# Reading the sampled outputs between two convolution taps, and a reordered start of the heads and of the sample turns, in a hybrid decoder step

## The reference

```
[cq | ckv | kr | z | xBC | dt | mq | g] = u @ w_in
A: latent attention, 8 heads, causal; the sampled tokens attend to a paged cache of 2048 old ones
B: conv of width 4 on xBC, silu; scan with state: y = C.S + ...; y = y + d_skip * x; gate by silu(z); norm
M: 4-head attention to 256 memory tokens
m  = sig(gA)*(oA@WoA) + sig(gB)*(oB@WoB) + sig(gM)*(oM@WoM);  x1 = LN(alpha*x + m@w_out)
y  = LN(alpha*x1 + relu(x1@w_up+b_up)^2 @ w_down + b_down)
```

## Time and profile before

| | us |
|---|---|
| median of 3 runs | 1730.83 |
| lowest, highest | 1729.92, 1733.96 |
| the profiled execution, its own time | 1732.98 |
| its span, first to last instruction | 1731.3 |

### The profile page before, as it was taken

One profiled execution on the slowest core, in us unless ns is written; L12 is line 12 of the kernel. 1 busy time (PEld: TensorE's weight loads), 2 busy tenths in 40 slices (PEclk: granted clock), 3 DMA queues, 4 the chain that ended last, 5 costly groups with the idle time before them and its releaser, 6 DMA issues.

```text
span 1731.3 us, 25873 instructions
## 1 busy us (share of the span) xinstructions
PE 1670.3 (96%) x10438; PEld 1411.0 (82%) x10438; DVE 760.8 (44%) x1312; ACT 408.3 (24%) x800; POOL 405.7 (23%) x344
## 2 busy tenths in 40 slices
PE   8999999999999999999999999999997999999995
PEld 6868777787877777777777767779996999999995
DVE  5567678675341211111221213343477871067334
ACT  2252433425211111111111101132224111111122
POOL 0041221404120000000333210013444443333432
PEclk9999999999999999999999999999998999999998
DMA  5324233252262222212677764432331222322211
GB/s 195 142 80 171 68 117 128 93 178 79 100 210 72 73 61 73 61 62 76 225 240 246 239 244 180 174 131 88 96 98 37 86 86 86 90 94 86 86 62 52
DMA packets 70409, 206.23 MB, mean 119 GB/s; under 512 B 10161, under 2 KB 26802, under 8 KB 65682
## 3 DMA queue, kind: packets, MB, share of 16 engines
q1 hardware_dynamic: 50384, 151.67, 26.8%
q10 hardware_dynamic: 13762, 31.93, 5.4%
q0 software_dynamic: 6144, 20.98, 3.9%
HBM read 189.68 MB, written 14.86 MB: 118 GB/s over the span
## 4 chain that ended last, share of the span: by engine, by line
PE 86%; DVE 8%; ACT 2%; DMA 2%; issue 2%; SPq 1%; POOLq 0%; POOL 0%; ACTq 0%; DVEq 0%
PE acc L1724 30%; PE acc L1764 29%; PE acc L2064 6%; PE acc L2030 3%; PE acc L2012 2%; PE acc L2167 1%; PE bank L2079 1%; PE bank L2098 1%; PE bank L2080 1%; DVE work L1212 1%; PE bank L2181 1%; PE bank L2049 1%; PE bank L2055 1%; PE bank L2252 1%; PE bank L1933 1%
## 5 line engine op out<-in xcount | busy, mean ns | idle before, releaser
L1724 PE MATMUL acc<-xt,ring 128*128 128x272 f32 x2272 | 546.7, 398 | 2.8 <-DMA ring<-in_stream 2.8
L1724 PEld LDWEIGHTS acc<-xt,ring 128*128 128x128 f32 x2272 | 428.6, 191 | 103.9 <-issue 18.6
L1764 PE MATMUL acc<-x_parts,f_parts 128*128 128x272 f32 x1408 | 220.9, 293 | 12.0 <-DVE x_parts L1141 10.8
L522 POOL TENSOR_TENSOR f_parts<-ring,f_parts 128x1024 fp32r<-128x1024 f32 x65 | 157.7, 2425 | 247.9 <-ACT f_parts L701 247.7
L1764 PEld LDWEIGHTS acc<-x_parts,f_parts 128*128 128x128 f32 x1408 | 197.5, 192 | 14.5 <-issue 8.0
L500 POOL DMA_DIRECT2D work<-in_page_cols x128 | 68.8, 538 | 474.4 <-PE bank L2119 365.3
L1764 PE MATMUL acc<-f_parts 128*128 128x272 f32 x1344 | 172.3, 289 | 0.0
L1764 PEld LDWEIGHTS acc<-f_parts 128*128 128x128 f32 x1344 | 170.4, 188 | 0.1
L701 ACT ACTIVATE f_parts<-ring 128x1024 fp32r<-128x1024 f32 x65 | 69.0, 1061 | 238.4 <-PE acc L1764 204.3
L2064 PE MATMUL acc<-branch,ring 128*128 128x272 f32 x512 | 120.0, 392 | 0.0
L2064 PEld LDWEIGHTS acc<-branch,ring 128*128 128x128 f32 x512 | 96.0, 190 | 18.8
(11 more groups left out here) (351 smaller groups left out, 2044.8 us busy)
## 6 DMA issues: line engine op xcount, KB each, us to landing
ring<-in_stream SPq DMA_DIRECT2D x216, 512.0 KB, 3.6
work<-in_page_cols POOLq DMA_DIRECT2D x128, 160.0 KB, 3.3
attended<-in_ssm_state ACTq DMA_DIRECT2D x8, 1024.0 KB, 6.3
work<-cum_rows SPq DMA_DIRECT2D x32, 256.0 KB, 4.6
out_ssm_s<-attended ACTq DMA_DIRECT2D x8, 1024.0 KB, 5.5
work<-in_ckv_rows ACTq DMA_DIRECT2D x64, 128.0 KB, 3.6
work<-in_ckv_rows SPq DMA_DIRECT2D x64, 128.0 KB, 3.0
work<-in_memk_cols SPq DMA_DIRECT2D x8, 1024.0 KB, 6.5
```

The source lines that it names most:

```text
L522: pool.tensor_tensor(lo, ring[:, s * BLOCK:(s + 1) * BLOCK], hi.bitcast(F), SUB).then_inc(sem["split_ready"], 1)
L1724: m = pe.matmul(acc[p][:, half, 0:width], w[:, k * P:(k + 1) * P], x(kk)[:, half * width:(half + 1) * width], start=kk == 0, stop=kk == n_ ...
L1764: m = pe.matmul(acc_half, w[:, k * P:(k + 1) * P], x[:, kk, of], start=kk == 0 and n == 0, stop=kk == last and n == 2)
```

## The change

Four edits, no arithmetic changed.

1. VectorE, groups 0 to 3: the read of the sampled outputs (line 1401) moves from behind `finish` of chunk 0 into the convolution of chunk 1, between its second and third tap operation of line 1212's loop (before `i == 2`). In group 3, where there is no convolution, it runs at the same place as a plain call.
2. SyncE: the first two weight blocks of the sample turns are loaded ahead of the first turn's rows; three instead of five follow them.
3. VectorE: the wait for all heads' sampled queries, the memset and `queries(0)` move ahead of the last head's merge (line 1510).
4. TensorE: the wait for `new_read` moves from ahead of `queries(0)` to behind its 24 matmuls, where the later heads wait for `q_lat_read`.

```diff
-            load(blocks_before("sample") - blocks_before("mem_k"))
+            load(blocks_before("sample") - blocks_before("mem_k") + 2)
...
             cached_rows(0)
-            load(5)
+            load(3)
...
-            def conv(g, q):
+            def conv(g, q, between=None):
...
                 for i in range(1, CONV_W):
+                    if i == 2 and between:
+                        between()
                     signal = "conv_done" if i == CONV_W - 1 else "dve_step"
...
-                def ahead(q):
+                def ahead(q, between=None):
                     if g < GROUPS - 1:
-                        conv(g + 1, q)
+                        conv(g + 1, q, between)
+                    elif between:
+                        between()
...
+                def read_y_s():
+                    dve.wait_ge(sem["y_s_ready"], t.next("y_s_ready"))
+                    for hp in range(GC):
+                        y = BR[:, g * GC + hp, SEQ:T]
+                        m = dve.scalar_tensor_tensor(out=y, in0=y, scalar=skip_of(hp), in1=bank[3][:,
+                                hp * NS:(hp + 1) * NS], op0=MUL, op1=ADD)
+                    m.then_inc(sem["y_s_read"], 1)
...
                 read_y(1)
-                ahead(1)
+                ahead(1, between=read_y_s)
                 ahead_finish(0)
-                dve.wait_ge(sem["y_s_ready"], t.next("y_s_ready"))
-                for hp in range(GC):
-                    y = BR[:, g * GC + hp, SEQ:T]
-                    m = dve.scalar_tensor_tensor(out=y, in0=y, scalar=skip_of(hp), in1=bank[3][:,
-                            hp * NS:(hp + 1) * NS], op0=MUL, op1=ADD)
-                m.then_inc(sem["y_s_read"], 1)
...
                 if h < MLA_HEADS - 1:
                     read_q_lat(h + 1)
+                else:
+                    dve.wait_ge(sem["q_lat_read"], t.next("q_lat_read", MLA_HEADS))
+                    dve.memset(q_rot_b, 0.0).then_inc(sem["dve_step"], 1)
+                    dve.wait_ge(sem["dve_step"], t.next("dve_step"))
+                    queries(0)
                 t.skip("acc0_ready"), t.skip("acc0_free")
...
-            dve.wait_ge(sem["q_lat_read"], t.next("q_lat_read", MLA_HEADS))
-            dve.memset(q_rot_b, 0.0).then_inc(sem["dve_step"], 1)
-            dve.wait_ge(sem["dve_step"], t.next("dve_step"))
-            queries(0)
...
             m.then_inc(sem["new_turned"], 1)
-            pe.wait_ge(sem["new_read"], t.next("new_read"))
...
                 pe.wait_ge(sem["acc0_free"], t.value("acc0_free") + 1)
-                if h:
-                    pe.wait_ge(sem["q_lat_read"], t.next("q_lat_read"))
+                pe.wait_ge(sem["q_lat_read" if h else "new_read"], t.next("q_lat_read" if h else "new_read"))
```

More of the change, by code:

```diff
@@ L1488, in read_q_lat, with queries @@
                         t=DEC_SEQ)).then_inc(sem["q_lat_read"], 1)
+            def queries(b):
+                one = bass.ds(b, 1)
+                for c in range(2):
+                    dve.tensor_scalar(q_lat_b[:, c, :], q_lat[:, c, one, :, :].rearrange("p b h t -> p (b h t)"),
+                            1.0, None, MUL).then_inc(sem["dve_step"], 1)
+                    dve.wait_ge(sem["dve_step"], t.next("dve_step"))
+                for h in range(2):
+                    of = slice(h * ROPE, (h + 1) * ROPE)
+                    signal = "batch_q_ready" if h else "dve_step"
+                    dve.tensor_scalar(q_rot_b[of, h, :], q_rot[of, one, :, :].rearrange("p b h t -> p (b h t)"),
+                            1.0, None, MUL).then_inc(sem[signal], 1)
+                    dve.wait_ge(sem[signal], t.next(signal))
             rotate_q()
```

## The result

| | before | after |
|---|---|---|
| median us | 1732.39 (4 runs, 1729.92 to 1733.99) | 1714.96 (4 runs, 1714.35 to 1717.8) |
| profiled execution, its own time | 1732.98 | 1717.8 |
| its span | 1731.3 | 1716.1 |

The ratio is 0.9902, with an interval of 0.9889 to 0.9914: 17.4 us less. Forecast were 1714.5, between 1709.5 and 1720.5. The profiled execution of after is the slowest of its four, 2.8 us over their median, and its gain over the profiled one of before is 15.2 us.

A forecast was written before the change was run, and what follows sets the result against it. TensorE, busy 1670.3 of 1731.3 us, bounds the kernel; only its stalls and lower-clock stretches can be won. 7.4 + 2.5 + 7.7 = 17.6 us gives 1715.4 (profiled) or 1713.2 (median); taken 1714.5, range 1709.5 to 1720.5.

The forecast's parts named there:

- part 1: SSM stage, sampled outputs read between the taps: state products stop waiting, 8.6 us less 3 x 0.4, so 7.4 us.
- part 2: Start of the heads, wait for new latents behind the first 24 matmuls: 2.5 us gained.
- part 3: Sample turns' start: first queries 1.9, weight loads 2.8, first projection at full clock 3.0; 7.7 us in sum.
- I take 0.4: SSM groups 0 to 2: VectorE's lateness returns as a wait for state sums, 0.4 us a group, range to 1.0.
- the 2.78 of group 1: SSM group 1: 2.78 us more than group 3 between projection half starts, counted as gain besides 1.17 of lower clock.
- rival 1: TensorE's clock losses move to remaining gaps instead of going: 13.4 us gained, 1719.6 us; chance 0.12.
- its cover: Heads' start: 24 matmuls take 5.77 us, ending near 505.0, so the latents' copy at 501.75 is in time.
- Both clock terms of the prediction: Lower-clock losses counted as gains: 1.2 us in SSM group 1 and 3.0 us in the first turn's projection.
- (2): Second sample turn: its key loads become the bound, wait of 1.7 plus up to 3.0 us, 1720.1; chance 0.06.
- (3): Line 1918: VectorE gives the SSM read's gain back at the next group's start, all 7.4 us, 1722.8; chance 0.05.
- (4): Slower than before: shifted work meets the clock monitor badly, 3.0 us per projection, eight give 1739; chance 0.02.
- (5): The moved read waits for something new or moved loads block SyncE's queue; only part 2 holds, 1730.5; chance 0.02.

The follow-up runs named there:

- e7: The changed kernel with the sampled-output read one tap earlier, ahead of tap 1: 1717.58 us, ratio 0.9909.
- e3: The kernel before with only the two weight-block loads moved ahead of the first sample turn's rows: 1727.65 us, ratio 0.9977.
- e4: The kernel before with only the first queries (wait, memset, queries(0)) moved ahead of the last head's merge: 1732.73 us, ratio 1.0003.
- e2: The kernel before with only the wait for the new latents moved behind the heads' first 24 matmuls: 1727.21 us, ratio 0.9968.
- e1: The kernel before with only the sampled-output read moved between the convolution's taps: 1724.99 us, ratio 0.9952.
- e6: The changed kernel with the sampled-output read behind all three taps, still ahead of chunk 0's finish: 1720.52 us, ratio 0.9928.
- a2: The changed kernel run again without edit: 1715.66 us, ratio 0.9906 against the kernel before.
- e9: e8 with TensorE's wait for the last memory values moved behind the first memory head's projection: 1711.67 us, ratio 0.9876.
- a3: The changed kernel run a third time without edit: 1714.98 us, ratio 0.9898 against the kernel before.
- e8: The changed kernel with the last four of the last turn's 16 key loads issued by SyncE, not GpSimd: 1714.37 us, ratio 0.9893.
- e8b: The e8 kernel run once more: 1714.03 us, ratio 0.9891.

## Why the prediction was right, and where it was off

The forecast was 0.5 us from the median. Point by point, the gains read between the two profiles up to the second turn:

| | predicted | measured | how |
|---|---|---|---|
| part 1 | 7.4 | 8.4 | turned latents at 498.63, now 490.39, and 0.14 for the later start of group 0 |
| part 2 | 2.5 | 2.45 | 501.81 - 498.63 = 3.18, now 0.73 |
| part 3 | 7.7 | 7.8 | 851.38 - 501.81 = 349.57, now 341.78 |
| behind it | 0 | -3.3 | 0.3 keys, 2.7 and 0.3 clock |

**Part 1, the term that was off** is "I take 0.4" for VectorE's lateness at the third convolution, three times: 0.07 to 0.09 came back, 0.24 in place of 1.2. VectorE reached the gating of chunk 0 at 128.50, 5.17 us after the half's start, where it took 5.99 in before: 0.8 earlier, not the 0.6 that I assumed. The taps cost 0.84 + 1.72 = 2.56 us for 3.22, which is the 0.6 to 0.7 expected; the other 0.2 are the read itself, which takes 125.92 - 125.28 = 0.64 from its start to the next tap's, and took 129.18 - 128.35 = 0.83 to the gating's. So the third convolution starts 8.93 us after the half, where with the wait's 2.33 taken off before it was 134.38 - 2.33 - 123.19 = 8.86: 0.07 late, and the products behind it are 0.07 late too. e7 shows what a little less would have cost: 0.76 late, 0.72 waited. The mechanism was right, its size was not. Of the sum of the gaps and of one clock loss, 8.6, nearly all came: 8.6 - 0.24 is the 8.4 measured. Two readings behind the term were not quite as written. The tap of 0.84 us was not one "without GpSimd beside it": GpSimd's multiply began at 124.79, in its middle. And the 2.78 of group 1 hold 0.45 us of lower clock besides the 1.17, since the two state products took 0.99 us to the next half's start where group 0's took 0.54; the sum is the same, but the clock's share of it is 1.6, so rival 1 should have read 13.0.

**Part 2** came as written; its cover held, since the copy at 493.10 is done long before the 24 matmuls end.

**Part 3** came as written, 1.9, 2.8 and 3.0. e3 and e4 add what the prediction did not say: its three terms are not independent. The queries' 1.9 us count only behind the loads', and alone they buy nothing, since TensorE then waits for weights by as much longer.

**The clock.** The prediction charged 4.2 us to it, 1.2 in the SSM stage and 3.0 in the first turn, and rival 1 said that these may move. Here is how long four places took in all profiles (TensorE, us; "gap" is TensorE's idle time before; bold: a part at 1.2 GHz). The last turn is taken from its first scores to the end of its first projection:

| profiles | SSM, half behind the state products, groups 0, 1, 2 | first turn, projection | last turn | first memory head |
|---|---|---|---|---|
| before | 3.83, **5.00**, 3.83 (gap 2.1) | **10.58** (gap 2.8) | **12.1** (gap 1.7) | 7.60 |
| e2 | **5.21**, 3.83, **5.25** (gap 2.1) | **9.26** (gap 3.2) | 10.5 (gap 1.4) | **10.28** |
| e3 | 3.83, 3.83, **5.52** (gap 2.1) | 7.60 (no gap) | 10.5 (gap 1.9) | 7.60 |
| e4 | 3.83, 3.83, **5.52** (gap 2.1) | **10.60** (gap 4.4) | **11.9** (gap 2.3) | **9.29** |
| e1 | 3.83 (no gap) | **10.53** (gap 2.9) | 10.5 (gap 2.1) | **10.23** |
| e6 | 3.83 (gap 1.3) | 7.60 | **12.2** (gap 2.1) | 7.60 |
| e7 | 3.83 | 7.60 | **12.2** (gap 1.8) | 7.60 |
| a2 | 3.83 | 7.60 | 10.5 (gap 1.6) | 7.60 |
| e9 | 3.83 | 7.60 | 10.5 (no gap) | 7.60 |
| after | 3.83 | 7.60 | **12.1** (gap 2.1) | **10.28** |
| a3 | 3.83 | 7.60 | 10.5 (gap 1.7) | **9.29** |
| e8, e8b | 3.83 | 7.60 | 10.5 (no gap) | **10.38**, **9.29** |

Where gaps of 2.1 us stood in the SSM stage, a stretch at 1.2 GHz followed one of them or two in 4 of 4 profiles, in another group from one to the next; without them, in none of 9. In the first turn it came in 4 of 4 with the wait for weights, and in none of 9 without it, e3's gap of 1.86 before the scores notwithstanding. The gap ahead of the heads' first projections was followed by the full rate in before, e3 and e4 (2.7 to 2.8, 24 matmuls in 5.77) and by the lower clock in e1 (3.04, 24 in 7.46), so a gap of this size makes the loss possible and not certain. Both clock terms of the prediction went with their gaps, and the choice to count them was right. Their sizes are those of one profile: e2 lost 2.8 us in the two projection halves of the SSM stage and 1.7 in the first turn.

Two places keep their gaps, and the loss there is a matter of chance. In the last turn it came in 5 of the 10 profiles with a wait for keys, 1.4 to 1.7 us each, and in none of 3 without; the profiles of before and after both have it, so it drops out of their difference, but it is part of what e8 and e9 remove. Ahead of the first memory head's projection stand a gap of 1.1 us, 3.7 us of scores, 3.65 of narrow matmuls (32 columns) and a gap of 0.5; there it came in 7 of 13. The profiled before was spared there, the profiled after was not, and that is the 2.7 us by which the profiled pair shows 15.2 rather than 18. By the prediction's own list this is a sign of being wrong, a granted clock below 1.00 in a new place, and it looks like rival 1. But e2 and e4 have the loss there as well with their clock losses in the SSM stage still in place, and a2, the same kernel as after, has not: it did not move, it comes and goes.

The Trainium skill's page "TensorE: Matmul & The Clock Gate", Part 1, has the monitor run freely and its cost vary from run to run. The traces agree for the first memory head (10.28, 7.60, 9.29 in one kernel) and for which group of the SSM stage is hit. What the prediction drew from it, that its 4.2 us may return at gaps that stay, they do not bear out: the gaps that stay lose clock in kernels with those 4.2 us and in kernels without.

**The base.** I took 1714.5, between 1715.4 from the profiled execution and 1713.2 from the median. The measured 17.4 us off 1732.39 is what the prediction's 17.6 expects. The split was luck in part: the median of before in later jobs was 1732.3 to 1733.7, 1.5 to 2.9 above the three runs I had.

**The rivals.** (1) see above; the measured total, 17.0 to 18.7 us in three comparisons, is not its 13.4. (2) No wait for keys at the second turn (832.90 has no bracket); the last turn's grew by 0.3, as the range had it in a small way. (3) TensorE's wait at line 1918, now 1925, is 2.4 us, from 2.5. (4) and (5) did not occur. Rival 4 counts two stretches at the lower clock, but the trace of before has more, at the last turn's scores (1008.96) and in the merge (granted 0.50 from 1306 to 1316), and so has that of after.

## What to carry to other kernels

When an engine reads something out that TensorE waits for, look for the spot inside its long steps, not only between them: e6 stands two taps later and loses 4.3 us by its trace, e7 one tap earlier and loses 1.9. Before two waits in a row are attacked, test whether the second just grows when the first goes (e4: nothing; with e3's loads: 1.9). And count the clock: a gap of 2 to 3 us in TensorE's work cost up to 3.0 more behind it in some executions and nothing in others, so removing it can pay twice, while a loss that comes and goes at some other place must be looked for before two single profiles are subtracted.

## What was not expected

GpSimd issues a key load every 1.15 us, but in the last turn the second comes after a gap of 3.15 us for which the profile's views show no cause. It stands at the same load in all 13 profiles, at 988.32 in before and 969.84 in after. By the times it is what makes this turn's keys late: in after's third turn the last load is issued 4.9 us before the scores start (853.93 and 858.86) and nothing waits; in the last turn the scores would follow the last load (986.28) by 2.4 us, and wait 2.06. No run without the gap tests it. From the timeline of GpSimd in before:

```profile
984.63 0.54 POOL L500 DMA_DIRECT2D work<-in_page_cols  x1 [7.84 <-PE bank L2119]
988.32 0.55 POOL L500 DMA_DIRECT2D work<-in_page_cols  x1 [3.15 <-issue]
989.48 0.54 POOL L500 DMA_DIRECT2D work<-in_page_cols  x1 [0.61 <-issue]
```

What the gap is stays open. A tap of 128 x 600 on VectorE that started while GpSimd multiplied took 1.47 us (before, the second of group 0) and 1.60 (e7, the first), and 0.84 otherwise, even where GpSimd's multiply began in its middle. The small read from PSUM took the same 0.72 beside GpSimd (in after, 125.28, inside GpSimd's 125.06 to 126.11) as it did alone.
